# Two passes of a loop turn interleaved: gate/up of both, then down of both

## The reference

```
h = x*(1+scale_f)+shift_f
for each token: best of 4 expert groups, in it the best 2 of 8 experts   (32 experts, two per token)
expert e of a row:  (silu(row @ w_g[e]) * (row @ w_u[e])) @ w_d[e]       (w_g, w_u 1024x256, w_d 256x1024)
x = LayerNorm(alpha*x + gate_f * (sum over the token's two experts of weight * expert row))
```

## Time and profile before

| what | us |
|---|---|
| median of 3 runs | 1648.49 |
| lowest and highest run | 1648.45, 1649.04 |
| span of the profiled execution | 1645.8 |
| PE busy in it | 1496.8 (91%) |
| DVE, ACT, POOL busy | 605.0, 355.9, 371.5 |
| chain that ended last: PE, DMA | 65%, 20% |

### The profile page before, as it was taken

How to read it: one execution, slowest core, us unless ns; L and a number is a source line. 1 busy time by engine, 2 the same in 40 slices (tenths; PEclk the granted TensorE clock), 3 DMA queues, 4 the chain that set the end, 5 groups by cost and what they waited for, 6 DMA issues and landing times.

```text
span 1645.8 us, 23813 instructions
## 1 busy us (share of the span) xinstructions
PE 1496.8 (91%) x8901; PEld 1044.6 (63%) x8901; DVE 605.0 (37%) x1452; ACT 355.9 (22%) x912; POOL 371.5 (23%) x491
## 2 busy tenths in 40 slices
PE   6999999998998998887999999999798899988774
PEld 4889889675887433332588989967487754334231
DVE  1301333766366211111450133466629732111116
ACT  2111111664001111110141111256411111111003
POOL 1000033522542121110110001453256132112100
PEclk8999999999998999998999999999999999999887
DMA  9321112774606999998522111176160579999934
GB/s 370 90 79 59 38 57 74 266 269 162 263 39 255 406 420 419 420 367 337 199 85 66 57 61 62 38 267 252 41 256 26 218 298 420 419 421 406 378 129 173
DMA packets 75761, 356.30 MB, mean 216 GB/s; under 512 B 21153, under 2 KB 24481, under 8 KB 40833
## 3 DMA queue, kind: packets, MB, share of 16 engines
q1 hardware_dynamic: 41184, 291.58, 45.0%
q0 software_dynamic: 21888, 48.83, 8.4%
q10 hardware_dynamic: 12576, 14.37, 2.6%
HBM read 344.37 MB, written 33.12 MB: 229 GB/s over the span
## 4 chain that ended last, share of the span: by engine, by line
PE 65%; DMA 20%; DVE 5%; POOL 3%; issue 3%; ACT 1%; SPq 1%; ACTq 0%; POOLq 0%; DVEq 0%
PE bank L995 24%; PE bank L1342 11%; DMA ring<-in_w_exp 7%; DMA z<-in_w_exp 6%; PE bank L1224 4%; PE bank L1361 4%; DMA hT<-in_w_exp 3%; PE bank L739 2%; PE bank L1147 2%; PE bank L775 2%; PE bank L1121 2%; DMA att<-mod_rows 2%; DMA att<-bias_full 1%; DMA z<-in_w_ada 1%; PE bank L766 1%
## 5 line engine op out<-in xcount | busy, mean ns | idle before, releaser
L995 PE MATMUL bank<-ring,hT 128*128 128x256 f32 (+1 forms) x1920 | 411.5, 374 | 2.4 <-ACT hT L1458 2.4
L995 PEld LDWEIGHTS bank<-ring,hT 128*128 128x128 f32 x1920 | 353.4, 191 | 47.4 <-issue 2.9
L1342 PE MATMUL bank<-ring,att 128*64 128x512 f32 (+1 forms) x448 | 181.9, 625 | 11.9 <-DMA z<-in_w_exp 10.2
L1342 PE MATMUL bank<-z,att 128*64 128x512 f32 (+1 forms) x416 | 167.2, 625 | 21.0 <-DMA hT<-in_w_exp 10.6
L1224 PE MATMUL bank<-ring,hT 128*128 128x256 f32 x640 | 142.9, 382 | 1.6 <-ACT hT L1620 1.1
L2728 POOL DMA_INDIRECT expert_rows<-att,cur x38 | 38.7, 1018 | 422.4 <-DVE att L2441 402.9
L1224 PEld LDWEIGHTS bank<-ring,hT 128*128 128x128 f32 x640 | 121.0, 191 | 17.8 <-issue 1.9
L2428 DVE TENSOR_TENSOR att<-att,bank 128x256 f32<-128x256 f32 x38 | 16.0, 421 | 312.7 <-ACT att L1704 312.7
L1342 PEld LDWEIGHTS bank<-ring,att 128*64 128x64 f32 (+1 forms) x448 | 60.1, 155 | 84.3 <-issue 82.2
L1342 PEld LDWEIGHTS bank<-z,att 128*64 128x64 f32 (+1 forms) x416 | 54.9, 152 | 81.4 <-issue 80.6
L1361 PE MATMUL bank<-z,att 128*64 128x512 f32 (+1 forms) x208 | 85.2, 625 | 12.2 <-DMA ring<-in_w_exp 12.2
(11 more groups left out here) (382 smaller groups left out, 2190.0 us busy)
## 6 DMA issues: line engine op xcount, KB each, us to landing
ring<-in_w_exp SPq DMA_DIRECT2D x84, 1024.0 KB, 18.7
z<-in_w_exp SPq DMA_DIRECT2D x78, 1024.0 KB, 19.9
ring<-in_w_ada SPq DMA_DIRECT2D x41, 1024.0 KB, 5.8
ring<-in_w_in SPq DMA_DIRECT2D x24, 1024.0 KB, 5.0
hT<-in_w_exp SPq DMA_DIRECT2D x20, 1024.0 KB, 18.4
att<-in_w_exp SPq DMA_DIRECT2D x10, 1024.0 KB, 22.0
z<-expert_rows ACTq DMA_DIRECT2D x20, 512.0 KB, 8.0
ring<-in_w_out SPq DMA_DIRECT2D x8, 1024.0 KB, 7.1
```

What stands on the lines that cost most here:

```text
L995: last = eng.matmul(bk[:, i * UN:i * UN + nw], hTv[:, k, t * P:(t + 1) * P], w[:, k, 0:nw], start=(k == 0), stop=(k == KD - 1))
L1342: last = eng.matmul(bank[2 + j][c * m_:(c + 1) * m_, :], e["xT"][:, j, k * P + c * m_:k * P + (c + 1) * m_], wv[c][:, :, k, :], start=(k = ...
```

## The change

The helper `passes` takes a function `turn(p, q)` for the loop beside `body` for the written-out passes, and each engine gets its own order for the two passes of a turn. On PE gate/up of q moves ahead of down of p, and the x of the pass after the turn moves to its end. ACT and DVE follow in the same order. On POOL the order in a turn is what it was. SP is not touched. The written-out passes keep their order; what else changes in `one_pass` is that tests for the loop case fall away.

```diff
-        def passes(eng, l, body, rest=None):
+        def passes(eng, l, body, rest, turn):
...
             with eng.Fori(0, more) as i:
-                body(Count(i, 2, PASSES))
-                body(Count(i, 2, PASSES + 1))
+                turn(Count(i, 2, PASSES), Count(i, 2, PASSES + 1))
...
                 def one_pass(b_):
                     block_gu(b_)
                     block_x(b_ + 1)
-                    if isinstance(b_, int):
-                        if b_ > 0:
-                            block_down(b_ - 1)
-                        block_hT(b_)
-                    else:
-                        block_hT(b_)
-                        block_down(b_)
+                    if b_ > 0:
+                        block_down(b_ - 1)
+                    block_hT(b_)
+
+                def turn(p, q):
+                    block_gu(p)
+                    block_x(q)
+                    block_hT(p)
+                    block_gu(q)
+                    block_down(p)
+                    block_hT(q)
+                    block_down(q)
+                    block_x(q + 1)
...
+                def turn(p, q):
+                    evac_sig(p)
+                    evac_x(q)
+                    evac_sig(q)
+                    evac_out(p)
+                    evac_out(q)
+                    evac_x(q + 1)
...
+                def turn(p, q):
+                    hidden(p)
+                    evac_x(q)
+                    evac_hT(p)
+                    hidden(q)
+                    evac_out(p)
+                    evac_hT(q)
+                    evac_out(q)
+                    evac_x(q + 1)
...
+
+                def turn(p, q):
+                    gather(p + 2)
+                    scatter(p)
+                    gather(q + 2)
+                    scatter(q)
```

More of the change, by code:

```diff
@@ L536, in program @@
             "wgu0", "wgu1", "wgu2", "wgu3", "wgu4", "wd0", "wd1", "wd2", "wd3", "wd4")} for l in range(DEPTH)]
-        def passes(eng, l, body, rest=None):
+        def passes(eng, l, body, rest, turn):
             for b_ in range(PASSES):
                 body(b_)
-            if rest is not None:
-                rest(PASSES - 1)
+            rest(PASSES - 1)
             eng.wait_ge(*ev.at("ctl", l))
@@ L1376, in one_pass @@
                     block_x(b_ + 1)
-                    if isinstance(b_, int):
-                        if b_ > 0:
-                            block_down(b_ - 1)
-                        block_hT(b_)
-                    else:
-                        block_hT(b_)
-                        block_down(b_)
+                    if b_ > 0:
[10 more added lines that the diff above has]
+                    block_x(q + 1)
                 keep_busy(22)
                 block_x(0)
-                n = passes(eng, l, one_pass, block_down)
+                n = passes(eng, l, one_pass, block_down, turn)
                 keep_busy(36)
@@ L1715, in one_pass @@
                     evac_x(b_ + 1)
-                    if not isinstance(b_, int):
-                        evac_out(b_)
-                    elif b_ > 0:
+                    if b_ > 0:
                         evac_out(b_ - 1)
+                def turn(p, q):
[5 more added lines that the diff above has]
+                    evac_x(q + 1)
                 evac_x(0)
-                n = passes(eng, l, one_pass, evac_out)
+                n = passes(eng, l, one_pass, evac_out, turn)
                 eng.wait_ge(W["scat0"], now(pair_count(n - 1) + 16))
@@ L2451, in one_pass @@
                     evac_x(b_ + 1)
[L2452 to L2459, removed]
+                    if b_ > 0:
+                        evac_out(b_ - 1)
+                    evac_hT(b_)
+                    if b_ == 0:
                         weights_of_two()
@@ L2733, in one_pass @@
                     gather(b_ + 2)
-                    if isinstance(b_, int) and b_ == 0:
+                    if b_ == 0:
                         for t in range(NT - 2, NT):
@@ L2738, in one_pass @@
                             ld(m["gf"][:, g, :], mrow(g, 3), *(("ld_gf", l) if g else ("ld_gf", l, 0)))
-                    if not isinstance(b_, int):
-                        scatter(b_)
-                    elif b_ > 0:
+                    if b_ > 0:
                         scatter(b_ - 1)
-                    if l == DEPTH - 1 and isinstance(b_, int) and b_ == PASSES - 1:
+                    if l == DEPTH - 1 and b_ == PASSES - 1:
                         eng.wait_ge(W["gu"], last_pass(PASSES, NBUF - 1) + 1)
                         ld_ln(2, l, m["lnend"])
+                def turn(p, q):
[3 more added lines that the diff above has]
+                    scatter(q)
                 gather(0)
@@ L2750, in _ @@
                 nought[0] = eng.value_load(ctl[0:1, C_ZERO:C_ZERO + 1], min_val=0, max_val=1)
-                n = passes(eng, l, one_pass, scatter)
+                n = passes(eng, l, one_pass, scatter, turn)
                 eng.wait_ge(W[f"gath{parity(n)}"], now(pair_count(n) + 16))
```

## The result

The changed kernel takes 1631.46 us, the median of 4 runs (1628.71 to 1636.05), against 1648.47 us of the kernel before: a ratio of 0.9907, 95% interval 0.9883 to 0.9932, 17.0 us. Two later sets of runs gave 0.9894 (0.9870 to 0.9918) and 0.9917 (0.9890 to 0.9945), by the medians 16.2 and 13.5 us. Single runs of the changed kernel scatter by some 5 us to either side of their median; those of the kernel before reach from 1642 to 1656 over all sets. What an experiment did is therefore read from its turns in the trace first and from the medians second.

The account below looks back on a forecast made before the run. TensorE was taken to be held in each layer's single loop turn, at down of p waiting for weights, then at low clock. Gains of 8.2 + 7.2 + 1.6 = 17.0 us off 1648.49 gave 1631.5 us, range 1627.5 to 1638.5.

Parts of the forecast that it names:

- The turns: Loop turn on TensorE: down of q ends earlier, gaining 8.2 us in layer 0 and 7.2 us in layer 1.
- gap ahead of gate/up of q: TensorE's wait in the turn: near nothing in layer 0, 2 to 3 us in layer 1.
- down of p without a wait: In the turn, down of p no longer waits for a transfer and takes some 3.5 us in both layers.
- from the end of down of p to down of q: Gap on TensorE between the turn's two down blocks: 1.13 us.
- the last down weight of q: Transfer in the turn: lands at about 782.8 us in layer 0 and 1581.7 us in layer 1.
- The way behind: After down of q, scatter to combine: nothing holds the gain back; GpSimd's slack in layer 1 is 1.3 us.
- Rival C: Behind the turn, at scatter q on GpSimd: the gain is lost again, time 1648 us; chance 0.03.
- the idle time between filler and combine: Sign on TensorE: at most 1 us of idle time follows the filler matmuls.
- The moved step: Turning x of the next pass, moved behind down of q: costs nothing; 1.1 us a layer if its cover were gone.
- The term of 1.6 us at the combine: First 24 matmuls of layer 1's combine run at full clock instead of low clock: 1.6 us gained.
- A: Rival in the turn: q's gate/up weights land only with p's down weights; gain 2.4 us, time 1646.1 us; chance 0.10.
- B: Rival in the turn: clock stays low from gate/up of q through down of q; 9.9 us slower, 1658.4 us; chance 0.03.

Follow-up runs that it names:

- e1: Changed kernel with x of the next pass left between gate/up of q and down of p: 1639.1 us, run again 1634.3 us.
- e2: Kernel before with 18 filler matmul calls between the hidden turn of p and down of p: 1647.0 us, ratio 0.9984.
- e4: Kernel before with SyncE's loop issuing gate/up p, down p, gate/up q, down q: 1638.8 us, ratio 0.9947.
- c1: Changed kernel run again unaltered as yardstick: 1631.5 us against 1647.7 us of the kernel before.
- c2: Changed kernel run once more unaltered as yardstick of a later set: 1632.4 us against 1645.9 us of the kernel before.
- e3: Changed kernel with SyncE's loop issuing gate/up p, down p, gate/up q, down q: 1643.2 us, ratio 0.9966.
- e7: Changed kernel with 12 filler matmul calls ahead of gate/up of p: 1635.0 us.
- e9: Changed kernel with 12 filler calls ahead of gate/up of p and 6 ahead of gate/up of q: 1631.8 us.
- e6: Changed kernel with two turns of the loop in each layer instead of one: 1694.3 us, against 1709.3 us for the kernel before with two turns.

## Why the prediction was right

**The turns.** From the first matmul of p's gate/up to the end of down of q I had worked out 26.1 us in layer 0 (760.55 to 786.7) and 30.4 in layer 1 (1558.56 to 1589.0). The profile has 26.4 (763.76 to 790.19) and 30.3 (1549.38 to 1579.71). Each step came as told: no gap ahead of gate/up of q in layer 0 (0.14 us), one of 2.75 us in layer 1 with the clock falling (a granted clock of 0.55 in the stretch shown below, most of it at the 1.2 GHz level; gate/up 8.68 us), down of p without a wait, and 1.2 us from the end of down of p to down of q, where I had taken 1.13.

```profile
1562.90:1566.30 3.40, 3.40 (x10) 1.08 (x11) 0.00 (x0) 0.00 (x0) 0.00 (x0) 0.55 0.48 198
```

(columns as in the earlier trace rows). One reading was off without weight in the sum: the last down weight of q was put at 782.8 us in layer 0 by shifting layer 1, where the trace of before has it land at 781.0 (issued at 757.6, 23.4 us). That the waiting is the cause, and not something else that the edit did, is shown by the two runs with SyncE's order turned round.

**The number.** That sum and first median are both 17.0 us is luck in part. The other two sets gave 16.2 and 13.5 us. The turns gave 15.1 us up to the end of down of q and 15.7 up to the combine, where 15.4 were booked; the other 1.6 us of the sum are a term that was booked too high, as told below.

**The way behind.** GpSimd's copy of q's scatter indices ended at 790.41 and the scatter was issued at 791.90:

```profile
790.21 0.20 POOL L2740 COPY cur<-att 128x1 int32 x1
...
791.90 1.00 POOL L2744 DMA_INDIRECT expert_rows<-att,cur  x1 [1.49 <-DVE att L2451]
```

The slack is 1.5 us, 1.4 was expected. Rival C had no footing. One of the signs named was missed: the idle time between filler and combine was to be 1 us at most, and was 1.39 us in layer 0 (0.35 in layer 1).

**The moved step.** I booked it at nothing, because the old kernel has it under work that is waited for. That it is free at its new place is right. That it would have cost 1.0 us a layer at the old one, in the new order, stood in the expectation only; the runs give 1.2 us a layer, and 3.3 to 3.6 for both up to the start of the combine.

**The term of 1.6 us at the combine.** Its size was right in the profile (12.25 became 10.55 us). As a forecast for a median it was booked too high. Of the ten combines in the five profiles with x ahead of the last down (the kernel before, both runs of e1's kernel, e2, e4) four took over 12 us, the one of the earlier trace rows among them; of the twelve in the six profiles with x behind it (after, c1, c2, e3, e7, e9), none. The two-turn runs add none of two to the first count and one of two to the second: with x behind the last down, the combine of layer 1 came after 1.94 us of idle time and took 12.25 us (e6).

```profile
1652.19 12.25 PE bank L773 x24
```

So it is 4 of 12 against 1 of 14. The cause may well be the one that I gave, but by these counts, which are small, it is worth a quarter of 1.6 us in each layer, some 0.8 in all. That it was the idle time alone isn't shown: e7 and e9 had 2.1 to 2.3 us of it before the combine of layer 0 and kept their clock.

**The rivals.** A did not come about by itself, and when it was forced it gave 5.6 us in place of the 2.4 worked out: 3.0 us of it in the turns up to the end of down of q, 1.7 at the combine of layer 1 (10.55 us for its first 24 matmuls), which I hadn't put into it, and the rest elsewhere. The Trainium skill's rule that the transfers of one engine need not complete in order (page "DMA: Bandwidth & Descriptors", section "Queues, rings and completion order") is borne out inside a group: of the four pieces of q's gate/up in layer 0, before, the one issued second (748.2) took 17.9 us and landed at 766.0, after the one issued third (748.7), which took 13.8 and landed at 762.5.

```profile
ring<-in_w_exp SPq DMA_DIRECT2D x1, 1024.0 KB, 17.9
z<-in_w_exp SPq DMA_DIRECT2D x1, 1024.0 KB, 13.8
```

It was not what decided: the last piece of q's gate/up landed 4.9 to 5.0 us ahead of p's last down weight in both layers, before and after (before 771.1 and 776.0, after 774.3 and 779.2 in layer 0). B is refuted: the clock came back within gate/up of q.

## What to carry to other kernels

When an engine waits for a transfer and has other work whose inputs land earlier, put that work first: the gain is the wait plus the slow clock behind it, less what is left of both at the new place (here 17.3 less 4.5 us, and 2.3 more from a gap that the new order closed), and it can be read off a trace from three landing times. Check both orders, that of the need and that of the issue, since turning round either gains (here 17.0 and 8.7 us) and turning round both gains less (5.6). In a loop that the transfers pace, such a gain is had once, behind the last turn, and not in each one.

## What was not expected of the hardware

- Filler matmuls that shortened a step ahead of a wait bought nothing here: 1.5 to 1.7 us won at gate/up of p came back as a longer wait for the next weights (0.14 us became 1.6 in layer 0, 2.75 became 4.2 in layer 1).
- The idle time alone does not tell whether the granted clock falls, as these durations of gate/up show (8.7 to 8.8 us after a fall, 7.1 without). Ahead of gate/up of q in layer 1 it fell after 1.97 us (c2), 2.75 us (after) and 2.9 us that followed 1.5 us of filler (e9), and held after 1.21 us (c1) and 2.71 us (e4, where a whole down block stood right before the wait and not the two short turns).
- The stretch from the combine of layer 0 to the first scatter of layer 1 has the same instructions in all kernels, and took from 539.8 to 550.4 us in the eleven profiles with one turn. When two are laid over each other matmul by matmul, most of the steps between them are 0.6 to 2 us, about what a stretch at low clock costs a block (1.6 us at the combine); that the clock makes them isn't shown. The time of one run of this kernel carries that scatter.
